# A three-block language-model stack on one core: gates spread over row groups, table loads and splits reordered, idle products at two norms

## The chip, the core and the metric

The kernel runs on one core of a Trainium2 chip. A time is what the device needs for one execution, in microseconds (us). The core has five engines that run their own instruction streams and meet at semaphores: TensorE (PE, matrix products), VectorE (DVE), ScalarE (ACT), GpSimd (POOL) and SyncE (SP), which here only issues DMAs. Lower is better.

## The reference

256 tokens of width 1024 pass through two layers of a first block, a norm, and one layer of a second block, all in float32.

```python
for layer in range(2):                                  # first block
    x = x + 0.5 * swiglu(rmsnorm(x), gate, up, down)    # hidden width 2816
    x = x + hybrid_mixer(rmsnorm(x), ...)
    x = x + 0.5 * swiglu(rmsnorm(x), gate, up, down)
x = rmsnorm(x, norm_final)
# second block
u = rmsnorm(x, g_pre_mix)
proj = u @ w_in                                         # 12 800 columns
mixed = sigmoid(gr + b) * (retention(rope(rq, rk), rv) @ w_ret_out) \
      + sigmoid(ga + b) * (dilated_attention(aq, ak, av) @ w_dil_out)
x = x + rmsnorm(mixed @ w_o, g_post_mix)
x = x + rmsnorm(square(relu(rmsnorm(x) @ w_up)) @ w_down, g_post_mlp)
x = x + rmsnorm(sigmoid(rmsnorm(x) @ w_ple_gate + b) * (p @ w_ple_in), g_post_ple)
```

The hybrid mixer joins three recurrences. The one that matters here is the gated delta rule over four heads. Each token has a gate per head, `beta = sigmoid(gd_b)` and `g = -exp(a_log) * softplus(gd_a + dt_bias)`. `g` is summed along the tokens, `decay = exp(cum[t] - cum[s])` multiplies the keys' products, and `beta` scales rows. Queries and keys go through a causal convolution, silu and an L2 norm (divided by the root of their sum of squares). The softplus is a logarithm of an exponential.

## The kernel before

**Data.** Activations lie transposed, features on the 128 partitions and the 256 tokens (`T`) along the free dimension. Products have float32 accuracy from three products each in a faster format: weights are split into a high part `w_hi` (ScalarE, L1368, 1.9 us a panel) and a low part `w_lo` = weight minus high part (VectorE, L1809, 2.3 us), and so are activations (`u_hi`, `u_lo`; `op_hi`, `op_lo`). TensorE computes high times high, high times low and low times high.

**Panels.** Weights come in 271 panels of 1 MB (a few are smaller). SyncE loads each into one of three `raw` slots as soon as that slot's last panel has been split. Two split slots hold the high and low parts, so the split of panel p waits until TensorE has finished panel p-2. A column panel gives 256 outputs in one of three banks `colb`, used in turn: TensorE may start panel p once panel p-3 has been evacuated. A row panel adds into the four banks `acc`. A panel keeps TensorE busy for 5.8 us.

**Order of work.** `schedule` is one list of steps that the host writes out in advance (`ffn` L408, `mixer` L436, `second_block` L533). Every engine walks through the whole list and does its own part of each step, strictly in order. `split_hi_to(p)` on ScalarE (L1373) and `split_lo_to(p)` on VectorE (L1814) bring the splits up to panel p. They are called at each panel (for p+1, L1402) and ahead of some steps; ahead of those named in `AHEAD` on both engines.

**Norms.** Ahead of a block, `pre_norm` starts the first two panels on `x` times the gain (`op_hi`), before the norm is known; their result is scaled afterwards. Meanwhile the sum of squares goes over TensorE, ScalarE takes the logarithm and the exponential for the reciprocal root, VectorE forms `u` (L1893), ScalarE `u_hi` (`fill` L1552), VectorE `u_lo`. After the fill ScalarE evacuates the first panel, with a table load ahead of it where the function needs another table. Three norms stand behind a product and ahead of an update of `x`, and one ahead of the second block; in these (`inside`) ScalarE first loads the table of logarithm and exponential (`ln_exp_tables` L1457), then squares the four banks, while VectorE multiplies by the gain (L1955), copies the strip of partial sums (L1909) and then updates `x` (L1928, L1929).

**The mixer around the gates.** The order is: a panel of the third recurrence; six panels of queries, keys and values (`gd_panel`), each with the convolution of the one before (`gd_conv`: VectorE taps, ScalarE silu and squares); the gates' panel of eight rows behind the second of them. `gate_rows` adds the bias (VectorE) and computes on ScalarE the sigmoid, then the absolute value, exponential, sum and logarithm of eight rows by 256 tokens (L1580 to L1589), with two table loads of their own before the next silu; `gate_log` and `gate_cum` (L2008, L2014) finish on VectorE and write `gates_c`. `gd_ss` (L1047, L1600) sums the squares and takes the roots. `rg_gates` computes gates of the third recurrence. `spread` (L1066) multiplies eight one-hot matrices `sel` of 8 rows with `gates_c`, so that each gate row stands on all 128 partitions of `acc`. VectorE forms the differences (L2034), ScalarE exponentiates (L1640), and only then may TensorE write the keys' products into `acc` (`gd_scores` L1077), which VectorE multiplies by the decays (L2096) as soon as it has issued its steps `hg_cum` and `hg_exponents`.

**The second block's start.** `ret_tables` (L788) has POOL load the positions and compute the angles of the rotary embedding, 24 small operations; `ret_sines` (L1723) is ScalarE's sine and cosine of them, placed after the sixth panel, with ScalarE waiting there for POOL.

**The MLP and the end.** `relu2` (L1851) squares an evacuated panel on VectorE. In the last block, four panels give gates; `ple` (L2343) multiplies them on VectorE, `ple_square` (L1547) squares the product on ScalarE, one panel later.

## Time and profile before

| | |
|---|---|
| median of 3 runs | 1819.59 us (1818.68 to 1823.10) |
| the profiled execution's own time | 1818.15 us |
| its span, first to last instruction | 1816.4 us |
| TensorE busy | 1754.7 us, 97% |
| TensorE weight loads | 1641.0 us, 90% |
| VectorE, ScalarE, POOL busy | 1082.0, 933.2, 102.1 us |
| mean granted TensorE clock | 0.99 of 2.4 GHz |
| read from HBM | 287.75 MB |

TensorE is busy nearly throughout, so the idle time ahead of its instructions is what to look for, and the granted clock, which halves in a few stretches: a busy TensorE at half the clock does half the work. An idle time of another engine costs something only where TensorE then waits for it. A float32 product that isn't in the split format shows as two records. Times such as 241.29 are us from the span's start. "issue" means that the profile shows no releaser.

### The profile page before, as it was taken

The page shows a single profiled execution, that of the slowest core. Times are in us where ns is not written, and L with a number is a line of the kernel's source. Part 1 is how long each engine was busy: PE and PEld are TensorE (multiplying, and loading weights), DVE is VectorE, ACT ScalarE, POOL GpSimd, SP SyncE. Part 2 cuts the span into 40 slices and gives each one's busy share as a digit, 9 for nine tenths or more (in the row PEclk, how much of TensorE's full clock was granted, in tenths as well). Part 3 has the DMA queues.
Part 4 walks back from the last instruction along what each step waited for, and adds up shares of the span by engine and source line. Part 5 has one row for each costly group of instructions (what it writes and reads, how often), then busy time and mean ns, then how long its engine had stood idle before and what let it go on. Part 6 is the DMA issues. An engine that isn't in the chain of part 4 may idle for free.

```text
span 1816.4 us, 32128 instructions
## 1 busy us (share of the span) xinstructions
PE 1754.7 (97%) x14072; PEld 1641.0 (90%) x14072; DVE 1082.0 (60%) x1266; ACT 933.2 (51%) x1033; POOL 102.1 (6%) x82
## 2 busy tenths in 40 slices
PE   8999999999999999999899999999999989999997
PEld 7999999899999999999899998889998779989986
DVE  5554688574456444698665446553465556765557
ACT  5433686563335433587563435544445454654445
POOL 0000001000000000001000000692000000000000
PEclk9999999999999999999999999999999999999998
DMA  7555462255554655562145555555255515455550
GB/s 250 185 189 185 150 185 71 71 170 185 191 186 151 200 186 189 157 183 97 67 139 191 185 186 161 180 194 200 71 186 179 169 37 173 162 170 190 190 170 24
DMA packets 206956, 290.87 MB, mean 160 GB/s; under 512 B 4608, under 2 KB 170624, under 8 KB 206688
## 3 DMA queue, kind: packets, MB, share of 16 engines
q1 hardware_dynamic: 206368, 287.04, 48.8%
q8 instruction: 111, 1.82, 0.4%
q0 software_dynamic: 448, 1.77, 0.3%
q14 instruction: 29, 0.24, 0.0%
HBM read 287.75 MB, written 1.05 MB: 159 GB/s over the span
## 4 chain that ended last, share of the span: by engine, by line
PE 84%; DVE 6%; ACT 6%; issue 3%; DMA 0%; SPq 0%; DVEq 0%; ACTq 0%
PE colb L842 55%; PE acc L842 27%; ACT w_hi L1368 2%; DVE u L1893 2%; DVE w_lo L1809 1%; PE aux L842 1%; DVE u_lo L1898 1%; PE acc L994 0%; DMA raw<-ffn_gate 0%; PE colb L1304 0%; ACT arena L1772 0%; DVE x L1929 0%; ACT L1459 0%; DVE u L1928 0%; ACT arena L1763 0%
## 5 line engine op out<-in xcount | busy, mean ns | idle before, releaser
L1809 DVE TENSOR_TENSOR w_lo<-raw,w_hi 128x2048 fp32r<-128x2048 f32 x271 | 625.6, 2309 | 499.9 <-ACT w_hi L1368 499.4
L1368 ACT ACTIVATE w_hi<-raw 128x2048 fp32r<-128x2048 f32 x271 | 516.3, 1905 | 368.2 <-PE acc L842 197.2
L842 PE MATMUL colb<-u_hi,w_hi 128*128 128x256 f32 x2256 | 302.1, 286 | 9.4 <-issue 6.1
L842 PEld LDWEIGHTS colb<-u_hi,w_hi 128*128 128x128 f32 x2256 | 286.9, 193 | 18.7 <-issue 9.2
L842 PE MATMUL colb<-u_lo,w_hi 128*128 128x256 f32 x2256 | 295.9, 284 | 0.0
L842 PE MATMUL colb<-u_hi,w_lo 128*128 128x256 f32 x2256 | 293.7, 283 | 0.0
L842 PEld LDWEIGHTS colb<-u_lo,w_hi 128*128 128x128 f32 x2256 | 283.2, 193 | 0.0
L842 PEld LDWEIGHTS colb<-u_hi,w_lo 128*128 128x128 f32 x2256 | 280.9, 192 | 0.0
L842 PE MATMUL acc<-op_hi,w_hi 128*128 128x256 f32 x544 | 98.4, 290 | 0.9 <-ACT arena L1686 0.9
L842 PE MATMUL acc<-w_lo,op_hi 128*128 128x512 f32 x384 | 95.6, 391 | 2.1 <-DVE w_lo L1809 2.1
L842 PE MATMUL acc<-w_hi,op_hi 128*128 128x512 f32 x384 | 96.5, 393 | 0.0
L842 PE MATMUL acc<-op_hi,w_lo 128*128 128x256 f32 x544 | 95.6, 284 | 0.3
L842 PE MATMUL acc<-op_lo,w_hi 128*128 128x256 f32 x544 | 95.0, 283 | 0.0
L842 PE MATMUL acc<-w_hi,op_lo 128*128 128x512 f32 x384 | 94.9, 389 | 0.0
L1429 ACT ACTIVATE act_t<-colb 128x512 f32<-128x512 f32 x44 | 26.2, 596 | 133.4 <-PE colb L842 129.0
L842 PEld LDWEIGHTS acc<-w_lo,op_hi 128*128 128x128 f32 x384 | 71.6, 188 | 19.1 <-DVE w_lo L1809 4.5
L842 PEld LDWEIGHTS acc<-w_hi,op_lo 128*128 128x128 f32 x384 | 72.1, 188 | 15.0
L842 PEld LDWEIGHTS acc<-op_hi,w_hi 128*128 128x128 f32 x544 | 80.0, 195 | 1.5 <-ACT arena L1686 1.2
L842 PEld LDWEIGHTS acc<-w_hi,op_hi 128*128 128x128 f32 x384 | 69.0, 189 | 12.5
L842 PEld LDWEIGHTS acc<-op_hi,w_lo 128*128 128x128 f32 x544 | 78.4, 192 | 0.7 <-DVE w_lo L1809 0.7
L842 PEld LDWEIGHTS acc<-op_lo,w_hi 128*128 128x128 f32 x544 | 78.5, 192 | 0.0
L842 PE MATMUL acc<-arena 64*64 64x64 f32 (+3 forms) x1448 | 64.6, 229 | 7.5 <-ACT arena L1772 2.6
(323 smaller groups left out, 1928.2 us busy)
## 6 DMA issues: line engine op xcount, KB each, us to landing
raw<-w_in SPq DMA_DIRECT2D x78, 1024.0 KB, 5.1
raw<-ffn_gate SPq DMA_DIRECT2D x44, 1024.0 KB, 5.3
raw<-ffn_up SPq DMA_DIRECT2D x44, 1024.0 KB, 5.3
raw<-ffn_down SPq DMA_DIRECT2D x44, 1024.0 KB, 4.9
raw<-w_up SPq DMA_DIRECT2D x16, 1024.0 KB, 5.3
raw<-w_down SPq DMA_DIRECT2D x16, 1024.0 KB, 4.9
raw<-w_out SPq DMA_DIRECT2D x8, 1024.0 KB, 5.0
raw<-w_ret_out SPq DMA_DIRECT2D x8, 1024.0 KB, 4.9
```

Of the source, the lines that this page charges most:

```text
L842: return pe.matmul(o, a, b, start=start, stop=stop, skip_group_check=True)
L1368: act.activation(split_view(w_hi, r), raw[:, p % RAW_SLOTS, 0:r["kt"] * r["nc"]], ACT.Copy)\
L1429: ins = act.activation(act_t[:, what[1] % 2, :], src, ACT.Silu)
L1809: tt(split_view(w_lo, r), raw[:, p % RAW_SLOTS, 0:r["kt"] * r["nc"]], split_view(w_hi, r).bitcast(F32), ALU.subtract).then_inc(sem("w_lo_r ...
L1893: ins = stt(u32[:, kk, :], x[:, kk, :], c(r["gain"], r["at"] + kk), rstd[:, :], ALU.mult, ALU.mult)
L1898: tt(u_lo[:, s, :], u32[:, s, :], u_hi[:, s, :].bitcast(F32), ALU.subtract).then_inc(sem("u_ready"), 1)
```

## The change

The one-hot matrices are written for four groups of 32 rows, two gates to a group, and a new step `gate_copies` multiplies `gates_c` (8 rows) by a matrix `copies` that repeats them at rows 0, 32, 64 and 96; ScalarE copies the result to `gates_4` (which shares `p32`). `spread` then multiplies in the order 0, 2, 4, 6, 1, 3, 5, 7, each product over 8 rows of its own row group, into four different banks in turn.

The exponential and logarithm of the gates leave `gate_rows` and stand in `gd_ss`, behind its table load; VectorE's `gate_log` moves from the fourth panel to behind the last convolution, and is in `AHEAD`.

ScalarE splits a third panel, p+3, right behind each fill. The table load of an inside norm stands ahead of the last row panel's split, or, in the last norm, behind the two last squares. `relu2` calls `split_lo_to` itself. POOL's angles wait for the fill's last `u_lo`, and the sines come one panel later. `ple_square` follows its own `ple`. Two inside norms, those not followed by the resident panel of `w_ple_in` and not the last, get eight products of `ones` with `ones` (128x128 each) into a free bank, behind the sum of squares.

```diff
--- before
+++ after
@@ -38,7 +38,7 @@
 
-AHEAD = ("gd_ss", "spread")
+AHEAD = ("gate_log", "gd_ss", "spread")
 EARLY = 2
@@ -56,7 +56,7 @@
           ("masks", 6 * HP), ("masks_t", 6 * HP), ("neg", P),
-          ("sel", 8 * P), ("sel_beta", 1), ("sel_g", 1), ("inv_freq", 1), ("freqs", DIL_HALF)]
+          ("sel", 8 * P), ("copies", P), ("sel_beta", 1), ("sel_g", 1), ("inv_freq", 1), ("freqs", DIL_HALF)]
 CONST_AT = {}
@@ -83,9 +83,12 @@
     sel = np.zeros((P, 8, P), f)
+    copies = np.zeros((P, P), f)
     for i in range(8):
-        sel[i, i] = 1
+        sel[32 * (i // 2) + i, i] = 1
+        copies[i, i::32] = 1
     put("sel", sel.reshape(P, -1))
+    put("copies", copies)
     rows = np.arange(P)[:, None]
@@ -144,6 +147,7 @@
         p32 = sb("p32", [P, 2, T])
+        gates_4 = p32[:, 0, :]
         arena = sb("arena", [P, 17450])
@@ -460,16 +464,16 @@
                     step("gate_rows", l=l)
-                if i == 3:
-                    step("gate_log", l=l)
                 step("gd_conv", l=l, i=i - 1, evac=e)
...
             step("gd_conv", l=l, i=5, evac=e)
+            step("gate_log", l=l)
             step("gate_cum", l=l)
...
             step("rg_gates", l=l)
+            step("gate_copies", l=l)
             e = cp(0, PC, "A", ("silu", hq))
@@ -542,11 +546,11 @@
 
-            step("ret_tables")
+            step("ret_tables", f=f)
             step("load_p")
...
                 e = cp(i * PC, "A", ("copy", rqk[:, 2 * i:2 * i + 2, :], 0))
-                if i == 5:
+                if i == 6:
                     step("ret_sines")
@@ -661,8 +665,8 @@
                 step("ple", i=i, evac=e, gain="g_post_ple_2")
-                if i:
-                    step("ple_square", i=i - 1, n=count["norm"] + 1)
+                if i < 3:
+                    step("ple_square", i=i)
             n = norm_sum("gated")
@@ -672,7 +676,7 @@
                 r["gained"] = next((w for w, _ in schedule[i + 1:] if w in ("gained", "norm_sum")), None) == "gained"
-        n_inside, n_first, last_x = 0, 0, None
+        n_inside, n_first, last_x, last_row = 0, 0, None, None
         for what, r in schedule:
@@ -690,6 +694,10 @@
                 r["inside"] = n_inside
+                if r["src"] != "gated":
+                    last_row["sums"] = r
+            if what == "panel" and r["kind"] == "row" and r["last"]:
+                last_row = r
         n_x, n_panels = count["x"], len(panels)
@@ -792,6 +800,7 @@
                 pool.wait_ge(sem("pos_loaded"), 16)
+                pool.wait_ge(sem("u_ready"), 4 * r["f"])
                 link(pool.tensor_copy(angt[:, 2, :], posf.bitcast(I32)))
@@ -1009,6 +1018,12 @@
 
+            def keep_warm(c, n):
+                col_bank_free(pe, c - 3)
+                for i in range(n):
+                    mm(colb[:, c % 3, 0:P], ones, ones)
             def tail_sums(r):
@@ -1029,6 +1044,8 @@
                 last.then_inc(sem("norm_summed"), 1)
+                if r["src"] != "gated" and panels[r["panel"]]["kind"] != "P":
+                    keep_warm(r["c"], 8)
 
@@ -1063,13 +1080,21 @@
 
+            def gate_copies(r):
+                l = r["l"]
+                pe.wait_ge(sem("gates_ready"), l + 1)
+                mm(aux[:, 0:T], k("copies", 0, P, 8), gates_c[:, :]).then_inc(sem("gates_turned"), 1)
             def spread(r):
...
                 l = r["l"]
-                pe.wait_ge(sem("gates_ready"), l + 1)
+                pe.wait_ge(sem("gates_copied"), l + 1)
                 pe.wait_ge(sem("rg_gates_read"), l + 1)
-                for i in range(8):
-                    mm(acc[:, T * i:T * i + T], k("sel", P * i, P, 8), gates_c[:, :])
+                o = CONST_AT["sel"]
+                for i in (0, 2, 4, 6, 1, 3, 5, 7):
+                    g = slice(32 * (i // 2), 32 * (i // 2) + 8)
+                    mm(acc[:, T * i:T * i + T], cst[g, o + P * i:o + P * i + P], gates_4[g, :])
                 for j in range(NT):
@@ -1399,11 +1424,14 @@
             def panel(r):
+                if r.get("sums"):
+                    ln_exp_tables()
                 split_hi_to(r["p"] + 1)
...
                         fill(r["fill"])
+                        split_hi_to(r["p"] + 3)
                 if r["kind"] == "W":
@@ -1501,7 +1529,6 @@
                     pair = r["src"] != "gated" and panels[r["panel"]].get("pair")
-                    ln_exp_tables()
                     for b in range(4):
@@ -1512,6 +1539,7 @@
                                 .then_inc(sem(("sq_half", "sq_ready")[t]), 1)
+                        ln_exp_tables()
                     if pair and r["src"] == "acc":
@@ -1581,12 +1609,7 @@
                 act.activation(gt[1], gt[0], ACT.Sigmoid).then_inc(sem("gates_sig"), 1)
-                ln_exp_tables()
-                link(act.activation(gt[3], gt[2], ACT.Abs))
-                link(act.activation(gt[4], gt[3], ACT.Exp, scale=-1.0))
-                link(act.activation(gt[8], gt[4], ACT.Identity, bias=one_row[0:8, 0:1]))
-                link(act.activation(gt[5], gt[8], ACT.Ln))
-                act.activation(gt[6], gt[5], ACT.Exp, scale=-1.0).then_inc(sem("gates_e"), 1)
+                act.activation(gt[3], gt[2], ACT.Abs).then_inc(sem("gates_abs"), 1)
 
@@ -1600,6 +1623,11 @@
                 ln_exp_tables()
+                act.wait_ge(sem("gates_abs"), l + 1)
+                link(act.activation(gt[4], gt[3], ACT.Exp, scale=-1.0))
+                link(act.activation(gt[8], gt[4], ACT.Identity, bias=one_row[0:8, 0:1]))
+                link(act.activation(gt[5], gt[8], ACT.Ln))
+                act.activation(gt[6], gt[5], ACT.Exp, scale=-1.0).then_inc(sem("gates_e"), 1)
                 act.wait_ge(sem("gd_ss"), l + 1)
@@ -1619,6 +1647,10 @@
                 ins.then_inc(sem("rg_tanh"), 1)
+            def gate_copies(r):
+                act.wait_ge(sem("gates_turned"), r["l"] + 1)
+                act.activation(gates_4[:, :], aux[:, 0:T], ACT.Copy).then_inc(sem("gates_copied"), 1)
 
@@ -1854,6 +1886,7 @@
                 tt(hid[:, n % 2, :], act_t[:, n % 2, :], act_t[:, n % 2, :], ALU.mult).then_inc(sem("hid_ready"), 1)
+                split_lo_to(r["panel"] + 1)
```

In the diff, functions of the same name occur once for each engine: `run` maps a step's name to the engine's function.

## Rows read from the trace of the kernel before

**Rows 1.** The page's busy shares, and TensorE's waits (total, times, longest)

```profile
PE 1754.7 (97%) x14072; PEld 1641.0 (90%) x14072; DVE 1082.0 (60%) x1266; ACT 933.2 (51%) x1033; POOL 102.1 (6%) x82
...
PE colb L842 <- issue: 6.1, 5, 2.1
...
PE acc L842 <- DVE w_lo L1809: 2.1, 5, 1.3
...
PE colb L842 <- ACT u_hi L1555: 1.4, 3, 0.7
...
PE colb L842 <- ACT w_hi L1368: 1.2, 4, 0.3
```

**Rows 2.** TensorE's timeline: start, duration, work, [idle before, and its releaser]

```profile
241.29 2.15 PE L842 MATMUL colb<-u_hi,w_hi 128*128 128x256 f32 x16 [2.06 <-issue]
...
1149.44 2.14 PE L842 MATMUL colb<-u_hi,w_hi 128*128 128x256 f32 x16 [1.22 <-issue]
...
1606.52 2.11 PE L842 MATMUL acc<-w_lo,op_hi 128*128 128x512 f32 x8 [1.31 <-DVE w_lo L1809]
```

**Rows 3.** ScalarE's timeline in mixer 0, at the gates' logarithm

```profile
233.71 0.42 ACT L1586 ACTIVATE arena<-act_t 8x256 f32<-8x256 f32 x1
...
235.58 1.28 ACT L1595 ACT_TABLE_LOAD   x1
...
239.27 1.92 ACT L1368 ACTIVATE w_hi<-raw 128x2048 fp32r<-128x2048 f32 x1
```

**Rows 4.** Timelines around the spread, and four column groups at a norm (1764.32)

```profile
275.40 4.07 PE L842 MATMUL acc<-gates_c,cst 8*128 8x256 f32 x16
...
1764.32 1.06 PE L842 MATMUL colb<-sq,one_row 128*32 128x256 f32 x12
...
275.51 0.60 ACT L1447 ACTIVATE arena<-colb 128x512 f32<-128x512 f32 x1 [0.93 <-PE colb L842]
...
277.94 2.29 DVE L1809 TENSOR_TENSOR w_lo<-raw,w_hi 128x2048 fp32r<-128x2048 f32 x1 [2.83 <-ACT w_hi L1368]
...
291.74 0.69 DVE L2096 TENSOR_TENSOR arena<-acc,arena 128x512 f32<-128x512 f32 x1 [1.31 <-PE acc L842]
...
844.82 0.68 DVE L2096 TENSOR_TENSOR arena<-acc,arena 128x512 f32<-128x512 f32 x1
```

**Rows 5.** Windows: stretch, length, PE busy (instructions), granted clock, DMA share, GB/s

```profile
280.00:290.00 10.00, 10.00 (x67) 0.73 0.33 107
...
1770.00:1780.00 10.00, 9.12 (x52) 0.66 0.03 7
```

**Rows 6.** POOL's and VectorE's timelines at the second block's first fill; a later fill

```profile
1132.89 1.25 POOL L795 CAST arena<-arena 128x256 f32<-128x256 int32 x1 [2.32 <-DMA arena<-positions]
...
1136.68 2.42 POOL L726 TENSOR_SCALAR arena<-arena 128x256 f32<-128x256 f32 x1
...
1161.74 0.85 POOL L735 TENSOR_SCALAR arena<-arena 128x256 f32<-128x256 f32 x1
...
1138.30 4.64 DVE L1893 SCALAR_TENSOR_TENSOR u<-x,cols,rstd 128x256 f32<-128x256 f32 x8
...
1785.93 3.25 DVE L1893 SCALAR_TENSOR_TENSOR u<-x,cols,rstd 128x256 f32<-128x256 f32 x8
```

**Rows 7.** Timelines at the norm ahead of the gated block

```profile
1760.66 1.28 ACT L1459 ACT_TABLE_LOAD   x1
1761.95 1.63 ACT L1500 ACTIVATE sq<-acc 128x512 f32<-128x512 f32 x3
...
1767.15 0.41 DVE L1909 TENSOR_SCALAR rstd<-colb 128x256 f32<-128x256 f32 x1
...
1770.88 1.50 PE L842 MATMUL colb<-op_hi,w_hi 128*128 128x256 f32 x4 [2.56 <-ACT op_hi L1482]
```

**Rows 8.** The keys' products (TensorE), and ScalarE's last logarithm

```profile
287.97 3.73 PE L842 MATMUL acc<-arena 128*128 128x128 f32 x32
...
1806.88 0.47 ACT L1463 ACTIVATE rstd<-aux,bias 128x256 f32<-128x256 f32 x1 [2.49 <-PE aux L842]
```

More of the change, by code:

```diff
@@ L1341, in dil_end @@
                 last.then_inc(sem("dil_o_turned"), 1)
-            run = {"panel": gemm, "acc_turn": acc_turn, "norm_sum": norm_sum, "gd_ss": gd_ss, "rg_gates": rg_gates,
+            run = {"panel": gemm, "gate_copies": gate_copies, "acc_turn": acc_turn, "norm_sum": norm_sum, "gd_ss": gd_ss, "rg_gates": rg_gates,
                    "spread": spread, "gd_scores": gd_scores, "gd_x0": gd_x0, "gd_y": gd_y, "gd_z": gd_z,
@@ L1779, in dil @@
                     turned(2 * p + 1)
-            run = {"panel": panel, "norm_sum": norm_sum, "acc_out": acc_out_, "ple_square": ple_square, "op_hi": op_hi_, "setup": setup, "gate_rows": gate_rows,
+            run = {"panel": panel, "gate_copies": gate_copies, "norm_sum": norm_sum, "acc_out": acc_out_, "ple_square": ple_square, "op_hi": op_hi_, "setup": setup, "gate_rows": gate_rows,
                    "gd_conv": gd_conv, "gd_ss": gd_ss, "rg_gates": rg_gates, "rg_scan": rg_scan, "spread": spread,
```

## The prediction

> **What bounds the kernel now.** I read the page's busy shares first, then TensorE's waits, then its timeline with each wait in place, then ScalarE, VectorE and the granted clock around those places. TensorE is busy 1754.7 of 1816.4 us [rows 1], so nothing beside it costs time unless TensorE stops for it or its clock is halved; some 62 us of idle and the halved stretches are all there is to win. The waits that this change touches: 6.1 us in five stops whose releaser isn't shown, 1.2 us in four stops for a high part of weights, 2.1 us in five for a low part, 1.4 us in three for `u_hi` [rows 1].
>
> The timeline puts them in place [rows 2]. Of the 6.1 us, 2.06 stand at 241.29 in the first mixer and as much (the longest are 2.1) at the same place in the second. ScalarE splits those weights only at 239.27 [rows 3], and TensorE starts as the split ends (239.27 + 1.92 = 241.19). Another 1.22 us stand at 1149.44; the last 0.8 are two short stops behind later fills, about 0.3 in the MLP and 0.5 in the gated block. Of the 2.1 us for a low part, 1.31 stand at 1606.52; the other 0.8 are four alike, one in each FFN.
>
> **The change, part by part.** The profiled execution took 1818.15 us (span 1816.4 plus 1.75 around it); the median of the runs, 1819.59, is 1.44 higher. The sum is made against 1818.15.
>
> *Gates' logarithm.* ScalarE loses, ahead of 239.27, one table load of 1.28 and four small operations from 233.71 to the load at 235.58, 1.86 together [rows 3]; that load, silu's, stays, since sigmoid, still in place, needs its own table. 3.1 us less covers the 2.06. DVE's part of the logarithm goes too. So everything behind comes 2.06 earlier in each mixer, as far as engines follow.
>
> The four operations return ahead of the keys' roots: +1.9 us on ScalarE, which then has only 0.2 of the 2.06 left through the gates' sigmoids and tanh. Behind those stands the new copy of the gates, about 0.4 (128x256 as 0.42 for a like operation at 233.71), so it is 0.2 later than before, where 0.93 us of idle ahead of 275.51 [rows 4] takes it in. The evacuation, its split and VectorE's subtraction at 277.94, which waits for that split, thus come only 0.2 to 0.7 earlier: 0.56 in my working. VectorE reads the spread gates only behind this subtraction. TensorE's new product of the gates (one of 8 rows: 4.07/8 = 0.5 us) finds its input about 0.5 us before it gets there: no wait, but little room.
>
> *Row groups.* Eight products over 8 rows take 4.07 us [rows 4]. Spread over four groups and four banks they should overlap: the nearest row is the sums of squares with 32 columns each, twelve records in 1.06 us, against sixteen in 4.07: a quarter of the time each. So 1.1 us, saving 2.9; bounds 0 (in turn) and 2.9. The Trainium skill ("TensorEngine Tiling (Array Packing)", Key Properties) says that different tiles run in parallel and that a change of mode drains the engine; by that it would be 1.1 plus a drain that no row shows for row groups. I take 1.1, but it hardly enters the sum: VectorE, held by 277.94, starts on the result no sooner, and TensorE has one more panel (5.8 us) before it needs VectorE's and ScalarE's answer. TensorE will stand before the keys' products for some 3.8 us.
>
> What counts is VectorE's product at 291.74, which had waited 1.31 us for TensorE in layer 0, and at 844.82 in layer 1, which had not [rows 4]. Gains: 0.56 + 1.31 = 1.9 and 0.56.
>
> The granted clock averages 0.73 over 280 to 290 [rows 5]: it was at its lower level (1.2 GHz) for over half of that, right behind the eight 8-row products. With a quarter of their time that fall should go, but a stop of 3.8 us can bring another: around 1770.88 [rows 7], where TensorE had waited 2.56 us, the clock averages 0.66 over ten [rows 5]. VectorE's slack hides most of it. I subtract 0.7: mixers 1.7 together. Bounds 0 and 4.2 (both waits saved in full).
>
> *Third split ahead of the evacuation, after each fill.* It takes away the 0.3 us stop and the 0.2 behind it in four FFNs (1.2 + 0.8 = 2.0), the 1.22 at 1149.44 and the two short ones of 0.3 and 0.5. Its cover: the evacuation comes up to 1.3 us later (a split of 1.92 in a gap of 1.1 behind a table load), while TensorE needs that bank one panel later, with 0.6 us or more to spare.
>
> *POOL's angles wait for the fill.* They ran under it, from 1132.89 to 1162.59, and `u` took 4.64 us there, where the fill at 1785.93 takes 3.25 [rows 6]. Two of the three stops for `u_hi` follow from it and go: 1.2. In return the angles start 11 us later, at about 1144, and with one more subtraction in their way end at about 1174. The sines stand one panel later, but ScalarE then splits for the panel that TensorE wants at 1175.9 of this scale; 1174.1 + 0.75 + 1.92 = 1176.8: 0.9 lost, bounds 0 and 3. So this norm: 1.22 + 1.2 - 0.9 = 1.5.
>
> *VectorE's split in the MLP.* 1.31 at 1606.52, since the subtraction no longer waits behind `op_lo`; with the short stop of 0.3: 1.6.
>
> *Norm before the gated block (1760s).* The table load at 1760.66 leaves the path to the squares: they start 1.29 earlier than 1761.95, VectorE's strip at 1767.15 follows by as much, and so does the operand that frees TensorE at 1770.88 [rows 7]: 1.3. At the norm of 1120 the last square waits for a split instead: 0. At that of 1566 TensorE has a panel to do: 0 to 0.3, taken as 0.
>
> *Idle products.* Eight of 128x128; by 32 records in 3.73 us, two to a product, they take 1.8 us [rows 8], inside waits of which the one at 1770.88 is 2.56 [rows 7] and the other 0.4 shorter: nothing, and 3.6 in all if nothing covered them. Their use is the clock, which averages 0.66 over 1770 to 1780 [rows 5]: a third of ten, 3.3 us of full-speed work, lost. I take these 3.3 as won; bounds 0 and 3.3.
>
> *The end.* The table load moves from ahead of the two last squares to behind them, and one square comes earlier. ScalarE, however, now waits twice for VectorE's gating, and the last evacuation comes 0.6 later. The logarithm at 1806.88 [rows 8] comes 0.7 to 1.9 earlier, by whether the clock falls: 1.3. The rows show 1.28 to a load [rows 7]. The Trainium skill ("ScalarE: Activation LUTs", What ACT_TABLE_LOAD costs) adds a drain of 1.38 to it. By that the two norms would give 2.8 more. The square behind the load at 1760.66 starts at 1761.95, 1.29 later [rows 7]: the trace doesn't agree.
>
> **Sum**: 2.0 + 1.7 + 1.5 + 1.6 + 0.5 + 1.3 + 3.3 + 1.3 = 13.2. 1818.15 - 13.2 = 1805. The clock's falls vary from run to run, and the median was 1.44 above; I add 1: 1806.
>
> **The rivals.**
> A. *The clock takes it back.* The idle products don't hold it (3.3), and the new stops before the keys' products bring a fall in each mixer that reaches past VectorE's slack (1 each). For it: the fall came where TensorE was busy all the time with 8-row products, so being busy isn't enough. Against it: 1.8 us of full-width work now stand in a stop of 2.56, and the stop is itself no longer than it was. 1806 + 5 = 1811.
> B. *The mixers pay in full.* VectorE isn't held by 277.94, and the groups' 2.9 and the clock's 3.3 come through in part, 2.5 more in each: 1801. Against it: the subtraction is put ahead of the spread in the program's order.
> C. *The row groups don't overlap.* Products in turn, the same fall of the clock: 2 lost in layer 0, 1.5 in layer 1, and the added 0.5 each: 1810.
> D. *Slower: POOL arrives late.* ScalarE is blocked at the sines until POOL's angles are there, and TensorE behind it. Had each of POOL's 24 operations the 2.5 us of those that a subtraction slowed (2.42 at 1136.68 [rows 6]), they would end at 1204: 31 lost, 1836. It decides from 13 us of lateness on. Against it: only those that met a subtraction were slow, one in 5.8 us.
>
> **Chances.** Forecast 0.52, A 0.2, B 0.1, C 0.1, D 0.03, and 0.05 for gains under 5.5 us by several terms at their lower bounds. 0.3%, about what a measurement of this kernel can tell from no change, is 5.5 us: under 1814.1 (1819.59 less 5.5) counts as faster. Forecast, B, C and nearly all of A lie there: 0.88; same 0.09; slower 0.03. The range takes in B and A with the runs' spread: 1800 to 1812.5.
>
> **What would show it.** TensorE's waits: no 2 us stop in the mixers' convolutions, none of 0.3 behind the FFNs' fills, 1606's gone; but a new one of 3 to 4 us before the keys' products, released by ScalarE's exponentials. Sixteen records of the spread in some 1.1 us. ScalarE's squares before the last norms 1.3 earlier. Clock at its upper level after 1770. The forecast is wrong if the mixers' spans shrink by over 4 us each, if TensorE stops over 2 us behind the sines, or if the idle products delay an operand's first use.

## The result, and the profile after

The changed kernel takes 1802.27 us (median of 4 runs, 1799.29 to 1804.52), the kernel before 1820.46 beside it: a ratio of 0.9898, 95% interval 0.9878 to 0.9918. The profiled execution took 1801.35 us, with a span of 1799.5. Between the two profiled executions lie 16.8 us, where the sum said 13.2.

The page of the changed kernel, its busy shares:

```profile
PE 1744.5 (97%) x14108; PEld 1634.6 (91%) x14108; DVE 1085.0 (60%) x1266; ACT 932.3 (52%) x1033; POOL 102.8 (6%) x82
```

And its waits of TensorE (total, times, longest), the largest and those that answer to [rows 1]:

```profile
PE acc L851 <- ACT small L1674: 6.2, 2, 3.1
...
PE colb L851 <- ACT arena L1470: 1.9, 1, 1.9
...
PE colb L851 <- ACT w_hi L1393: 1.4, 2, 1.1
...
PE acc L851 <- DVE w_lo L1841: 0.2, 1, 0.2
PE colb L851 <- ACT u_hi L1583: 0.2, 1, 0.2
```

The 6.1 us without a shown releaser are gone, so is nearly all of the waiting for low parts and for `u_hi`. What is new is 6.2 us in two stops of 3.1: the one forecast before the keys' products. Of the 1.4 for a high part, 1.1 stand at the kernel's first weights, 0.3 behind the sines. One stop of 0.2 for a low part is left, in the MLP, where 1.31 stood at 1606. TensorE is busy 10.2 us less, 5.5 of it in the two spreads (4.07 and 3.72 before, 1.15 each now).

TensorE's timeline of the changed kernel in mixer 0, the lines that answer to [rows 4, 8]:

```profile
273.19 1.15 PE L851 MATMUL acc<-p,cst 8*128 8x256 f32 x16
274.16 0.23 PE L1099 MATMUL aux<-cst,gates_c 8*128 8x8 f32 x2
274.32 2.17 PE L851 MATMUL colb<-u_hi,w_hi 128*128 128x256 f32 x16
276.33 2.08 PE L851 MATMUL colb<-u_lo,w_hi 128*128 128x256 f32 x16
278.25 2.08 PE L851 MATMUL colb<-u_hi,w_lo 128*128 128x256 f32 x16
283.44 5.47 PE L851 MATMUL acc<-arena 128*128 128x128 f32 x32 [3.11 <-ACT small L1674]
```

The spread takes 1.15 instead of 4.07. The Trainium skill ("TensorEngine Tiling (Array Packing)", Key Properties) says that tiles run in parallel and that a change of mode drains the engine; the first holds here, and for the second the panel behind the spread takes 2.17 where its next group takes 2.08, so no drain of any size shows. What the row groups save, TensorE spends standing: 3.11 before the keys' products, which then take 5.47 instead of 3.73, at the lower clock. VectorE's timeline of the same place shows why it stands:

```profile
273.39 0.43 DVE L2108 TENSOR_SCALAR arena<-arena 128x512 f32<-128x512 f32 x1
276.01 2.29 DVE L1841 TENSOR_TENSOR w_lo<-raw,w_hi 128x2048 fp32r<-128x2048 f32 x1 [2.19 <-ACT w_hi L1393]
278.22 0.17 DVE L2063 COPY small<-aux 128x16 f32<-128x16 f32 x1
...
281.63 1.36 DVE L2166 TENSOR_SCALAR arena<-arena 128x512 f32<-128x512 f32 x1
...
288.94 0.69 DVE L2129 TENSOR_TENSOR arena<-acc,arena 128x512 f32<-128x512 f32 x1 [0.46 <-PE acc L851]
```

The spread's result lies ready from 274.4 and VectorE reads it at 278.22, behind the low part's subtraction, as forecast.

**Stretch by stretch.** Executions of one kernel differ by up to 5 us, mostly by 1 to 3, as much as most parts of this change are worth; where profiles differ in stretches that no edit touches, it is by falls of the clock and by the wait for the first weights. A finer measure is the stretch between fixed points of TensorE's timeline. The table gives the times between the first sums of squares of one norm and of the next, in the profiled execution of each kernel (us; the experiments are told below). "In turn" means the spread as before, from one group of rows.

| stretch (time after at its end) | before | after | E1 no third split | E2 no idle products | E3 in turn | E4 logarithm alone | E5 angles early | E6 loads as before | E12 |
|---|---|---|---|---|---|---|---|---|---|
| start, FFN (210) | 211.19 | 210.44 | 212.64 | 210.86 | 212.51 | 211.10 | 210.39 | 210.49 | 210.19 |
| mixer 0 (377) | 169.98 | 166.82 | 166.54 | 166.41 | 166.31 | 165.70 | 166.76 | 167.32 | 165.68 |
| FFN (568) | 192.25 | 191.16 | 192.30 | 191.15 | 191.16 | 192.26 | 191.15 | 191.15 | 191.15 |
| FFN (760) | 192.28 | 191.16 | 192.27 | 191.17 | 191.15 | 192.28 | 191.15 | 191.16 | 191.15 |
| mixer 1 (926) | 167.75 | 166.59 | 168.18 | 167.61 | 165.68 | 165.97 | 167.14 | 166.68 | 167.58 |
| FFN (1112) | 186.53 | 185.40 | 186.51 | 185.38 | 185.39 | 186.51 | 185.38 | 185.39 | 185.39 |
| norm (1126) | 14.00 | 14.01 | 13.99 | 15.14 | 14.01 | 15.36 | 14.00 | 14.00 | 14.00 |
| second block's mixers (1555) | 432.74 | 429.75 | 431.95 | 429.65 | 429.68 | 432.75 | 430.47 | 429.65 | 429.67 |
| norm (1572) | 16.31 | 16.32 | 16.30 | 16.31 | 16.30 | 16.31 | 16.30 | 16.31 | 16.30 |
| MLP (1751) | 181.29 | 179.57 | 180.21 | 179.58 | 179.60 | 181.33 | 179.59 | 179.58 | 179.59 |
| norm (1765) | 17.29 | 14.15 | 14.14 | 15.15 | 14.14 | 16.05 | 14.15 | 15.57 | 14.14 |
| gated block (1786) | 20.28 | 20.55 | 21.66 | 20.54 | 20.53 | 20.27 | 20.53 | 19.57 | 19.54 |
| end | 14.46 | 13.60 | 11.97 | 11.96 | 11.97 | 13.31 | 11.97 | 14.38 | 12.05 |

Stretches that no edit touches repeat to 0.02 or 0.03 us where the clock doesn't fall (to 0.1 in the second block's mixers). The first one (weights from a cold start) and those with a fall vary by 1 to 2.

### The profile page after: what moved, and what is told of

Same layout as the page of the kernel before. It is cut to its first block, busy times and chain, and to the rows that moved or that the text cites. A ratio compares the mean times of both kernels' runs of the same rounds, so it can differ in the third digit from the quotient of the medians.

```text
span 1799.5 us, 32199 instructions
## 1 busy us (share of the span) xinstructions
PE 1744.5 (97%) x14108; PEld 1634.6 (91%) x14108; DVE 1085.0 (60%) x1266; ACT 932.3 (52%) x1033; POOL 102.8 (6%) x82
## 4 chain that ended last, share of the span: by engine, by line
PE 82%; ACT 7%; DVE 6%; issue 2%; POOL 2%; DMA 0%; SPq 0%; DVEq 0%; ACTq 0%; POOLq 0%
PE colb L851 53%; PE acc L851 27%; ACT w_hi L1393 2%; DVE u L1926 2%; PE aux L851 1%; DVE w_lo L1841 1%; PE acc L1003 0%; DMA raw<-ffn_gate 0%; DVE x L1962 0%; ACT arena L1804 0%; POOL arena L741 0%; DVE u L1961 0%; ACT L1487 0%; PE colb L1329 0%; ACT L1475 0%
```

## The experiments

**E1: the third split.** Its edit:

```diff
                     if r["half"] == 0:
                         fill(r["fill"])
-                        split_hi_to(r["p"] + 3)
```

> The changed kernel without ScalarE's third split ahead of the evacuation behind each fill. The first theory: a stop costs more than the idle time printed beside it, since the printed idle runs from the modelled end of the last product and the first product behind it is slow again; so the 0.3 us stop for the high part and the 0.2 for the low part come back in each of four FFNs and cost 0.52 and 0.57, 1.1 together, the stops of pre-mix and gated block come back too, and the whole is 6 us slower than the changed kernel (about 1808), with each FFN block from its norm's sums to the next FFN's again 1.1 longer. The rival: the stops cost what is printed (0.5 in each FFN) and the rest of the FFNs' gain has another cause, which stays: 3.5 us slower (about 1806), FFN blocks 0.5 longer.

Measured: 1807.92 us (1807.37 to 1810.45), ratio 0.9941 (0.9926 to 0.9956): by the medians 5.7 slower than the changed kernel. Each FFN is 1.11 to 1.14 longer again, as before the change. Its TensorE's timeline behind the fill, the same place as in the kernel before:

```profile
390.73 2.08 PE L851 MATMUL colb<-u_lo,w_hi 128*128 128x256 f32 x16
393.11 2.15 PE L851 MATMUL colb<-u_hi,w_hi 128*128 128x256 f32 x16 [0.30 <-ACT w_hi L1393]
395.10 2.08 PE L851 MATMUL colb<-u_lo,w_hi 128*128 128x256 f32 x16
...
398.94 2.08 PE L851 MATMUL acc<-w_hi,op_hi 128*128 128x512 f32 x8
401.22 2.14 PE L851 MATMUL acc<-w_lo,op_hi 128*128 128x512 f32 x8 [0.20 <-DVE w_lo L1840]
403.20 1.08 PE L851 MATMUL acc<-w_hi,op_lo 128*128 128x512 f32 x4
```

The changed kernel there:

```profile
388.82 2.08 PE L851 MATMUL colb<-u_lo,w_hi 128*128 128x256 f32 x16
390.74 2.08 PE L851 MATMUL colb<-u_hi,w_hi 128*128 128x256 f32 x16
392.66 2.08 PE L851 MATMUL colb<-u_lo,w_hi 128*128 128x256 f32 x16
...
396.50 2.00 PE L851 MATMUL acc<-w_hi,op_hi 128*128 128x512 f32 x8
398.34 1.98 PE L851 MATMUL acc<-w_lo,op_hi 128*128 128x512 f32 x8
400.15 1.98 PE L851 MATMUL acc<-w_hi,op_lo 128*128 128x512 f32 x8
```

Read the starts, not the brackets. From one group to the next it is 1.92 us without a stop, though each is printed as 2.08: the records overlap by 0.16. With the stop it is 2.38, and the group behind it takes 1.99: 0.53 lost where 0.30 is printed. At the low part it is 2.28 and 1.98 for 1.84 and 1.81: 0.61 where 0.20 is printed. The first theory holds: a short stop costs its bracket, the overlap of 0.16 (0.24 at the low part) and 0.1 to 0.2 of slower first products. That was the forecast's largest miss, 2.0 for 4.5.

Beyond the FFNs E1 has a stop of 1.25 behind the sines where the changed kernel has 0.31, and one of 1.88 in the gated block where it has none and the kernel before 0.51. The changed order needs the third split there.

**E2: the idle products.** 

```diff
-                if r["src"] != "gated" and panels[r["panel"]]["kind"] != "P":
-                    keep_warm(r["c"], 8)
```

> The changed kernel without the idle products at the two norms. The first theory: the products held the clock in the gated block's norm, so without them the clock falls behind the stop at about 1755 (a mean of 0.66 to 0.75 over the ten us behind it), and that costs 1 to 2 us at TensorE's next product of the second panel, not the 3.3 that were forecast, since VectorE holds part of that stretch; at 1115 nothing changes. 1803 to 1804. The rival: the clock stays up without them, and the gain of that norm came from the table load and the fall that happened not to come: same time as the changed kernel, 1802, no fall in the trace.

Measured: 1803.27 us (1802.03 to 1803.90), ratio 0.9912 (0.9897 to 0.9927), which alone can't be told from the changed kernel. The stretches can: both norms, 1126 and 1765, are longer by 1.13 and 1.00. Of the others mixer 1 is 1.02 longer, where its fall is deeper (0.66 granted over 830 to 840, for 0.83 in the changed kernel), and the end 1.64 shorter, where the changed kernel has a fall (0.83 over 1780 to 1790). Windows of its TensorE (stretch, length, busy, granted clock, DMA share, GB/s):

```profile
1110.00:1120.00 10.00, 6.94 (x48) 0.91 0.24 82
1750.00:1760.00 10.00, 7.20 (x55) 0.99 0.35 120
1760.00:1770.00 10.00, 10.00 (x77) 0.83 0.01 2
```

The changed kernel's:

```profile
1110.00:1120.00 10.00, 8.72 (x67) 1.00 0.33 105
1750.00:1760.00 10.00, 8.59 (x66) 1.00 0.33 107
1760.00:1770.00 10.00, 9.33 (x83) 1.00 0.00 1
```

So the products hold the clock, and at both norms, not at the one; each is worth 1 us when the fall comes. In the eleven kernels here that have them no fall stands at either norm; in the three that don't (before, E2, E4) one stands at five of six. It need not come: the kernel before has 14.00 at 1126 without any. Nor do they delay an operand's first use, which comes 5.9 us after the sums at 1112 with and without them.

**E3: the spread in turn.** The extra product and the copy go, the selection matrices have their rows at 0 to 7 again:

```diff
-                pe.wait_ge(sem("gates_copied"), l + 1)
+                pe.wait_ge(sem("gates_ready"), l + 1)
...
-                for i in (0, 2, 4, 6, 1, 3, 5, 7):
-                    g = slice(32 * (i // 2), 32 * (i // 2) + 8)
-                    mm(acc[:, T * i:T * i + T], cst[g, o + P * i:o + P * i + P], gates_4[g, :])
+                for i in range(8):
+                    mm(acc[:, T * i:T * i + T], k("sel", P * i, P, 8), gates_c[:, :])
```

> The changed kernel with the gates spread as before: eight products of 8 rows in turn from one row group, without the extra product and ScalarE's copy. The first theory: TensorE has slack of 3.1 us before the keys' products, since VectorE and ScalarE end later than it; the products take 4.07 instead of 1.15 and end at about 277 instead of 274.2, ahead of the low part's subtraction on VectorE (to 278.2), so the stop before the keys' products shrinks from 3.1 to about 0.8 and the start of the keys' products stays within 0.3: no change in time, 1802, the row groups gain nothing. The clock falls in the spread instead of in the keys' products. The rival: the row groups are what brought the mixers' gain: 2 to 4 us slower, 1804 to 1806.

Measured: 1800.47 us (1800.15 to 1802.00), ratio 0.9900 (0.9883 to 0.9916). The rival is out: nothing is lost. TensorE's timeline of this kernel in mixer 0:

```profile
274.42 4.00 PE L850 MATMUL acc<-gates_c,cst 8*128 8x256 f32 x16
278.22 0.32 PE L1096 MATMUL aux<-cst,gates_c 8*128 8x8 f32 x2
278.47 3.78 PE L850 MATMUL colb<-u_hi,w_hi 128*128 128x256 f32 x16
282.05 3.18 PE L850 MATMUL colb<-u_lo,w_hi 128*128 128x256 f32 x16
285.06 2.08 PE L850 MATMUL colb<-u_hi,w_lo 128*128 128x256 f32 x16
286.98 3.73 PE L850 MATMUL acc<-arena 128*128 128x128 f32 x32
```

The clock falls behind the 8-row products and slows the panel (3.78, 3.18), in time that TensorE would otherwise stand; the keys' products then run at full speed with no stop. With row groups it stands 3.1 us, and the clock falls in the keys' products, which VectorE waits for. Over the six stretches in turn (E3, E4, E12) a mixer takes 166.15 on the mean, over ten with the row groups (after, E1, E2, E5, E6) 167.0: 0.85 more, where either kind spreads over 1.8 to 1.9. So the row groups don't gain here; by the stretches they lose somewhat, by the medians it can't be told.

**E4: the logarithm alone**, in the kernel before:

```diff
-                if i == 3:
-                    step("gate_log", l=l)
...
             step("gd_conv", l=l, i=5, evac=e)
+            step("gate_log", l=l)
             step("gate_cum", l=l)
```

with ScalarE's four operations moved to `gd_ss` and `AHEAD` as in the change.

> The kernel before with the move of the gates' logarithm alone (beside the keys' roots on ScalarE, its place on VectorE to match); spread in turn, all else as it was. The first theory: this move is the whole of the mixers' gain: the 2.06 us stops in the convolutions go, and a stop of some 1 to 2 us takes their place before the keys' products; from the norm of the first FFN's end to that of the mixer's (211 to 381 us) 3 us less in layer 0 and 1.5 in layer 1, 2 to 4.5 in all, so 1814.5 to 1817 against 1818.9. The rival: without the row groups the spread in turn is in the chain and takes it back: the mixers' stretches within 0.5 of before.

Measured: 1812.23 us (1811.00 to 1812.99), ratio 0.9956 (0.9939 to 0.9973). That is 8.0 less than beside it, more than expected. The mixers are 4.28 and 1.78 shorter than before, 6.1 together, more than in the changed kernel (3.16 and 1.16). The stop of 1 to 2 us that was expected before the keys' products doesn't come: the spread in turn and the slower panel behind it fill that time. The other stretches, whose code is untouched, make up the rest by falls that came or not. 1.2 of layer 0 is no part of it: the kernel before has a fall of the clock in the output panel, in its TensorE's timeline, that the others lack there:

```profile
329.66 3.65 PE L842 MATMUL acc<-op_hi,w_hi 128*128 128x256 f32 x16 [0.47 <-ACT arena L1686]
```

From the mixer's norm to this line the kernel before takes 118.47, E4 115.39, the changed kernel 116.50. In layer 1 it is 117.42, and 116.27 for the changed kernel. So the move alone brings the mixers' whole gain, and 1.1 us more in layer 0 and 0.6 in layer 1 than the change as a whole.

**E5: the angles at once**, and the sines behind the sixth panel (number 5 in the loop), as before:

```diff
-                pool.wait_ge(sem("u_ready"), 4 * r["f"])
```

> The changed kernel with GpSimd's angles running at once again (no wait for the fill) and the sines back behind the fifth panel. The first theory: the angles then share the fill's time with VectorE, whose operand takes 4.6 us there instead of 3.3, and TensorE waits again for its high part: the stretch from the sums of the norm at 1125.6 to the next at 1555.3 is 1.2 to 1.5 us longer, some 1803.5. The rival: the stops of that norm came from the clock or from the third split alone, and the place of the angles costs nothing: same as the changed kernel within 0.5.

Measured: 1801.76 us (1800.78 to 1801.98), ratio 0.9900 (0.9879 to 0.9920). The stretch from 1126 to 1555 is longer, by 0.72 against the changed kernel and 0.82 against E2, E6 and others, half of what was expected. Mixer 1 (0.55 longer) and the end (1.6 shorter) differ by falls of the clock. VectorE's timeline of E5 has the slow operand again, with GpSimd busy 9.23 of the ten us from 1130:

```profile
1130.29 4.64 DVE L1925 SCALAR_TENSOR_TENSOR u<-x,cols,rstd 128x256 f32<-128x256 f32 x8
```

The changed kernel's:

```profile
1129.90 3.25 DVE L1926 SCALAR_TENSOR_TENSOR u<-x,cols,rstd 128x256 f32<-128x256 f32 x8
```

**E6: the table loads and squares as before.**

```diff
-                if r.get("sums"):
-                    ln_exp_tables()
                 split_hi_to(r["p"] + 1)
...
+                    ln_exp_tables()
                     for b in range(4):
                         if b == 3 and pair and r["src"] == "x":
...
-                        ln_exp_tables()
...
-                if i < 3:
-                    step("ple_square", i=i)
+                if i:
+                    step("ple_square", i=i - 1)
```

> The changed kernel with ScalarE's table loads back ahead of the squares of the norms inside, and the squares of the last gated block one chunk later, as before. The first theory: at the gated block's norm (sums at 1751) the operand is again 1.3 us later, so the stretch to the next norm's sums grows from 14.15 by 1.3, or up to 3 if the clock then falls; at the two other norms within 0.3; and the end, which takes 32.5 us from the last norm's sums to the end where the clock holds, grows to 34: 2.5 to 4 us slower, 1804 to 1806. The rival: the end's 2 us between the kernels came from the clock alone and the norm's from the idle products, so nothing but 0.3 is lost.

Measured: 1802.94 us (1802.37 to 1803.46), ratio 0.9906 (0.9889 to 0.9922). The norm at 1765 is 1.42 longer, the two others are the same: the load's 1.28 and hardly more. The Trainium skill ("ScalarE: Activation LUTs", What ACT_TABLE_LOAD costs) adds 1.38 of drain to a load; by that the norm would be some 2.7 longer (an estimate from the page's figures), and the measurement, 1.42, decides against it. The end is 2.4 longer than the 12.0 that it takes elsewhere; E4, with the same order there, has 13.31, so 1.1 of it is put to the clock and 1.3 to the load; no run separates them. But the gated block is 0.98 shorter. That was not expected: the squares of one chunk *earlier* stand ahead of an evacuation on ScalarE, and TensorE waits for the last one. Its timeline in E6:

```profile
1786.87 1.15 PE L851 MATMUL colb<-sq,one_row 128*32 128x256 f32 x12 [0.93 <-ACT arena L1468]
```

and in the changed kernel:

```profile
1785.92 1.70 PE L851 MATMUL colb<-sq,one_row 128*32 128x256 f32 x12 [1.92 <-ACT arena L1470]
```

**E7 to E11: the stop before the keys' products.** If VectorE and ScalarE answered sooner, the stop of 3.1 would go. E7 swaps two steps of the mixer's order and leaves the low part's subtraction to the next panel:

```diff
+            step("spread", l=l)
             step("rg_scan", l=l)
-            step("spread", l=l)
...
-                if what in AHEAD:
+                if what in AHEAD and what != "spread":
                     split_lo_to(r["panel"] + 1)
```

E8 has the second of these edits, keeps the order and puts the subtraction right behind VectorE's spread:

```diff
                 if what in run:
                     run[what](r)
+                if what == "spread":
+                    split_lo_to(r["panel"] + 1)
```

> The changed kernel with VectorE's part of the spread no longer behind the next low part's subtraction, and ScalarE's exponentials of the gates ahead of the recurrence's logarithms. The first theory: the keys' products wait for that chain alone; VectorE starts it at 274.5 instead of 278.2, ScalarE ends it at about 280 instead of 283.4, TensorE finds it done as it gets there (280.2), and the stop of 3.1 is gone. But VectorE's own work up to the half products at 294.6 is nearly gapless behind, with 2.2 us of idle ahead of the subtraction to be won: 1.5 to 2.2 in each mixer, so 3 to 4 in all, 1798 to 1799, and a new stop of 1 to 2 us before the products of the halves. The rival: the recurrence's logarithms, now later, hold GpSimd and the end of the recurrence, and the stop moves behind without gain: 1802, or 1 to 2 slower.

Measured: 1807.27 us (1805.70 to 1807.94), ratio 0.9933 (0.9919 to 0.9948): 5 slower than the changed kernel.

> The changed kernel with the low part's subtraction on VectorE behind the spread instead of ahead of it; ScalarE's order stays, so GpSimd's recurrence is as early as in the changed kernel. The first theory: VectorE's idle 2.2 us ahead of the subtraction shrinks to about 0.7 and everything behind comes 1.5 earlier; ScalarE's exponentials begin when the recurrence's logarithms end (280.4 instead of 281.7), so the stop before the keys' products shrinks from 3.1 to 1.8 and the half products come 1.3 to 1.5 earlier: 2.5 to 3 us faster than the changed kernel in the two mixers, about 1799.5. Here the row groups count, since VectorE starts right behind them. The rival: VectorE's work slips under GpSimd's, which slows both on the port they share (1.1 us of an operation that takes 0.41 alone), and the gain is under 0.5, or a loss as in the kernel with the exponentials first.

Measured: 1801.14 us (1799.65 to 1802.77), ratio 0.9896 (0.9877 to 0.9915); mixers 166.13 and 167.56: nothing. E7's TensorE starts the keys' products without a stop, and then stands 2.57 and 2.16 before the half products, for VectorE. E8's VectorE has spread and subtraction behind it at 280.26, the changed kernel's at 281.63. It lost the lead here:

```profile
280.59 2.29 DVE L2169 TENSOR_TENSOR_SCAN arena<-one_row,u 128x256 f32<-128x256 f32 x2
...
283.50 1.49 DVE L2188 TENSOR_TENSOR sq<-arena 128x256 f32<-128x256 f32 x1
284.91 0.82 DVE L2187 TENSOR_TENSOR sq<-arena 128x256 f32<-128x256 f32 x1
285.65 0.41 DVE L2188 TENSOR_TENSOR sq<-arena 128x256 f32<-128x256 f32 x1
...
286.66 1.78 DVE L2125 TENSOR_TENSOR arena<-arena 128x512 f32<-128x512 f32 x1
```

The same operation takes 0.41 to 1.49. GpSimd's timeline of E8 has the recurrence there (279.55 to 287.9), one of its operations slowed too:

```profile
279.55 2.78 POOL L789 TENSOR_TENSOR arena<-arena 128x512 f32<-128x512 f32 x1 [4.15 <-ACT arena L1664]
```

So E9 holds the recurrence until VectorE has its exponents (with E7's order on ScalarE), E10 does the same with the changed kernel's order, and E11 is E9 with the spread in turn. All three have the subtraction behind the spread, as in E8:

```diff
             def rg_scan(r):
...
+                pool.wait_ge(sem("hg_de"), 8 * l + 3)
                 pool.wait_ge(sem("rg_tc"), l + 1)
```

> The changed kernel with the order of the kernel before this call's (the low part's subtraction behind VectorE's spread), ScalarE's exponentials of the gates ahead of the recurrence's logarithms, and GpSimd's recurrence held until VectorE has formed the first three exponents, so that the two no longer overlap in operations from SBUF alone. The first theory: what ate the gain of the last two orders was the overlap with GpSimd, under which VectorE's 0.42 us operations take 1.4; GpSimd's five to six operations now fall beside VectorE's operations on PSUM, which they don't slow much, and end by 294, ahead of their use at 299. So the keys' products start without a stop at about 280.2, and the half products at about 292 instead of 294.6: 2.5 to 3 us in each mixer, 5 to 6 in all, about 1796.5. The rival: VectorE's operations on half the partitions and from PSUM are slowed as well, or GpSimd is late for the recurrence's end; then the gain is under 1, or TensorE stops before the hierarchy's values.

> The kernel with the low part's subtraction behind the spread, and GpSimd's recurrence held as in the kernel sent with this one; ScalarE's order as in the changed kernel, so the keys' products wait for the recurrence's logarithms. The first theory: VectorE's slowed operations (3.4 us over their usual times in the first layer) give back 2.5 or more, the stop of 2.0 before the second half products goes to about 0.3, and the stop of 1.6 before the keys' products stays: 1.5 to 2 in each mixer against the kernel without the hold, about 1798. The rival: no overlap effect, the long operations are long for another reason: same as without the hold, 1801.

> The first kernel of this call with the gates spread in turn instead of in four row groups. The first theory: where VectorE takes the spread's result at once, the row groups are worth their 2.9 us less what VectorE can do in between; VectorE starts at 277 instead of 274.5, and the half products come 2 to 2.5 later in each mixer: 4 us slower than that kernel, some 1800.5. The rival: TensorE, with 2.9 us more of its own, is then the later one and the loss is the same 2.9 on TensorE; or the clock, which falls in the 8-row products, adds another 1 to 2 in each.

Measured: E9 1803.75 us (1802.02 to 1804.98), ratio 0.9913 (0.9898 to 0.9928); E10 1801.26 (1799.74 to 1803.10), 0.9900 (0.9883 to 0.9916); E11 1807.56 (1805.84 to 1808.45), 0.9934 (0.9919 to 0.9949). Both first theories on the hold fell. E10's mixers take 167.99 and 167.21, no less than the changed kernel's. The exponents are fast now (0.42 each), and the price has moved with GpSimd onto the operations that had been said to be hardly slowed. VectorE's timeline of E9:

```profile
284.92 1.15 DVE L2127 COPY small<-arena 128x4 f32<-128x4 f32 x1
...
286.69 3.19 DVE L2137 SCALAR_TENSOR_TENSOR arena<-arena 64x256 f32<-64x256 f32 x3
...
291.73 2.01 DVE L2137 SCALAR_TENSOR_TENSOR arena<-arena 64x256 f32<-64x256 f32 x3
```

These take 0.17, 1.28 and 1.28 elsewhere: 3.6 us more, as much as E8 had lost (3.8 in all, against the 1.26, 0.42 and 0.68 of E9). VectorE's last operand for the half products is ready at 294.65, in the changed kernel at 294.71, and TensorE now stands before it (2.88 us in E9), which lowers the clock behind. E11 gives the row groups' worth where VectorE waits for the spread: mixers 169.40 and 169.39 for 167.83 and 169.25, 1.6 and 0.1 rather than 2 to 2.5 each. The medians are 3.8 apart, close to the 4 expected, so the profiled executions don't show where the rest lies.

**E12.** E3 with the squares one chunk later, as in E6, and the load left behind the last two:

```diff
-                if i < 3:
-                    step("ple_square", i=i)
+                if i:
+                    step("ple_square", i=i - 1)
```

> The changed kernel with the gates spread in turn and, in the last gated block, the squares one chunk later as before the change, while the table load stays behind the two last squares. The first theory: in the kernel with both loads and squares as before, the last evacuation came as TensorE ended (0.9 us stop instead of 1.9), which was the later squares' doing, and the end lost 2.5, of which the load's place is 1.3 and a clock's fall the rest; so here the last block's sums come 1.0 earlier than in the changed kernel, the last square 0.5 earlier, and the end takes 32.0 us from the sums of the last norm's operand instead of 32.5. With the spread in turn that is about 1800.0 against the 1800.5 of that alone. The rival: the end is VectorE's gating and the last squares, which come no earlier: 32.5 again, 1800.5.

Measured: 1798.08 us (median of 5, 1796.79 to 1798.55), ratio 0.9878 (0.9859 to 0.9897); before beside it 1818.87. The gated block and the end take 31.59 where E3 has 32.50: 0.9 less, twice what was expected, since the end pays next to nothing for the later squares. It is the lowest median of all kernels here, 4.2 under the changed kernel's (3.6 by the ratios, each with its own measurement of the kernel before beside it); the two intervals overlap.

## Why the prediction was right, and where its terms were off

Forecast were 1806 us and the range 1800 to 1812.5, measured 1802.27. The total came so close partly because errors cancelled. Of the 16.8 us between the profiled executions the sum had 13.2; against its terms the third split gave 2.5 more, the mixers 2.6 more, the second block 1.5 more, the norm 1.5 less, gated block and end 1.2 less, the start took 0.4. And 1.9 of the gain (1.2 in mixer 0, 0.7 around 1450) is luck: falls that the profile of before has and that of the changed kernel doesn't. By its own steps:

- *Third split*, 2.0 in the FFNs: 4.5 (1.09, 1.12 and 1.13 in three, the fourth lies in the first stretch). The mechanism was right, shown by E1; the size was read from the brackets, which leave out the overlap of the records and the slow first products.
- *VectorE's split in the MLP*, 1.6: 1.72. By E1 the short stop behind the fill (0.3 in the forecast) gave 0.64 of it and the long one 1.08. That one shrank from 1.31 to 0.20; the forecast had it gone. No run takes VectorE's split out by itself.
- *Mixers*, 1.7, of it 1.9 and 0.56 less 0.7 of clock: 1.97 in layer 0 and 1.16 in layer 1 up to the output panel, 3.1 in all, and 1.2 more by a fall that was in the profile of before by chance. The term that was mis-sized is the 0.56: from the mixer's norm VectorE's subtraction starts 1.18 earlier in layer 0 (65.57 for 66.75) and 1.17 in layer 1. ScalarE's table load ahead of the evacuation at 275.51 starts 0.27 earlier (61.84 for 62.11) where the forecast had ScalarE 0.2 later, and the 0.93 of idle behind it is gone. Against that VectorE's product behind the keys' products, which was to wait no more, still waits 0.46 and 0.49 for the keys' products in their fall of the clock, 0.95 where 0.7 was put. Together that is 2.0 (1.18 + 1.31 - 0.46) and 0.7 (1.17 - 0.49); the other 0.5 in layer 1 comes behind the half products, where no run looked. The stop, its releaser (ScalarE's last exponential) and its place were as forecast; it is 3.1 where 3.8 was said. E4 shows that the logarithm's move is the whole of it.
- *Row groups*: that they hardly enter the sum was right, and by E3 they bring nothing. The spread took 1.15 for 1.1, but by luck: twelve records in 1.06 and sixteen in 4.07 are a third of the time each and not a quarter, which makes 1.4.
- *Second block's mixers*, 1.5: 2.3 up to the sines' panel, where TensorE stands 0.31 and not 0.9. The angles ended at 1165.0, 0.6 ahead of the forecast's 1174 less the 8.4 won up to there. E5 gives 0.7 to 0.8 to the wait. Another 0.7 is a fall around 1450 that the profile of the changed kernel doesn't have. The same code has it or not from kernel to kernel.
- *Norm and idle products*, 1.3 + 3.3: 3.1 together. E6 gives the load 1.4, as forecast. E2 gives the products 1.0 here and 1.1 at 1115, where the forecast had seen nothing to win. The latter is no part of the 16.8, since the kernel before had no fall there. The step that failed is that it took the clock lost over ten us (3.3) as lost time: behind a norm TensorE waits for operands anyway, and part of the half speed falls into those waits. Less the load's 1.4, the fall at 0.66 granted over ten us was worth 1.7; that of E2, at 0.83, was worth 1.0.
- *Gated block and end*, 0.5 + 1.3: 0.6 in this execution, which had a fall in the end (13.60 where eight of the other kernels have 12.0). With the clock up it would be 2.2. Inside, the third split gave 0.7 (20.28 before, 19.57 in E6, whose squares come as before), and the squares put one chunk earlier, which the forecast costed at nothing, took 1.0 back (E6, E12).
- *The start*: 0.4 lost at the first weights, within what the first stretch varies by.

Of the rivals, A (the clock) has its mechanism shown and its size wrong: the idle products do hold the clock, and the new stops do bring a fall, worth 0.4 to 0.5 in a mixer (166.82 with the fall; 166.41 in E2, whose keys' products took 3.84). B's premise, VectorE not held, was tried in E8 and brings nothing. C is out: the groups overlap, sixteen records in 1.15. D is out: the angles ended at 1165.0 and TensorE stood 0.31 behind the sines.

Open is what decides whether a given stop of 2 to 3 us is followed by a fall: E2 had one at 1115 and the kernel before, with the same wait, had none. And whether the row groups lose 0.85 by the copy (0.3 later on VectorE) or by the fall in the keys' products wasn't separated.

## What to carry to other kernels

Price a short stop of a pipelined engine by the starts of its instructions, with and without it: here 0.2 to 0.3 printed were 0.5 to 0.6 lost, and eight such stops together cost 4.5 us. An engine that is made faster where another holds the chain only stands longer, and the standing can cost clock: before a 2.9 us shortening, look at what the next engine is doing when the result is ready. And moving GpSimd's work in time didn't remove its interference with VectorE here; other operations paid, so sum it over the whole overlap before counting on it.

## What the runs showed of the hardware that was not expected

- VectorE beside GpSimd: an operation on 128x256 from SBUF took 0.41 alone and 1.49 beside GpSimd's products (E8), and three on 64 partitions 3.19 instead of 1.28. Over one recurrence (six GpSimd operations, of which the first stands apart in E8 and the changed kernel) VectorE lost 3.8 us in E8, 3.6 to 3.9 in E9 and 2.3 in the changed kernel (two operations of 1.36 for 0.42, and 0.4 in a scan), where part of it ran beside VectorE's reads of PSUM.
- Sixteen records of TensorE's idle products of 128x128, in a gap that is otherwise 2.2 to 2.6 us, went with stretches of 14.0 and 14.15 us at those norms in every kernel that had them (bar E6's load); the three without them (before, E2, E4) each have a longer one at one of the two at least.
- TensorE busy all the time with 8-row products was followed by a fall in E3: 0.77 granted over 280 to 290 with TensorE busy 10.00 of 10.
